# Expert gathers of a two-block transformer kernel: one token tile after the other, with blocks of 32 columns on TensorE in place of VectorE sums

## The reference, cut to what matters

```python
s1, i1 = lax.top_k(sc[:, :, 0], 16)
s2, i2 = lax.top_k(sc[:, :, 1], 16)
cand = s1[..., :, None] + s2[..., None, :]          # 16 x 16 sums a head
top_s, pos = lax.top_k(cand, 16)
idx = take_along_axis(i1 * 128 + i2, pos)           # 256 tokens x 8 heads x 16
gate = softmax(top_s)
act = gelu(einsum('chkd,cd->chk', u[idx], h))       # a dot product a row
out = einsum('chk,chkd->cd', gate * act, v[idx])    # a weighted sum of rows
x = x + out
```

## Time and profile before

| | |
|---|---|
| median of three runs | 2830.98 us |
| the profiled execution: first to last instruction | 2833.1 us |
| expert stage, first u gather to the last add into `x` | 515.6 to 1336.3 us |
| GpSimd busy over the whole span | 820.1 us |
| VectorE busy | 1396.1 us |
| TensorE busy | 2141.6 us |
| mean granted TensorE clock | 0.873 of full speed |

### The profile page before, as it was taken

How to read it: one execution, slowest core, us unless ns; L and a number is a source line. 1 busy time by engine, 2 the same in 40 slices (tenths; PEclk the granted TensorE clock), 3 DMA queues, 4 the chain that set the end, 5 groups by cost and what they waited for, 6 DMA issues and landing times. The chain is left out here.

```text
span 2833.1 us, 25536 instructions
## 1 busy us (share of the span) xinstructions
PE 2141.6 (76%) x9580; PEld 1041.9 (37%) x9580; DVE 1396.1 (49%) x2952; ACT 424.9 (15%) x914; POOL 820.1 (29%) x902
## 2 busy tenths in 40 slices
PE   7976797867836656655999799988889986655664
PEld 5544343734412222222655333322236453222222
DVE  3478434979997677776564422211146443101011
ACT  1322100112200211111222301000011131000000
POOL 3325433548777677775010000000000000000000
PEclk9986898978967777778999899999999997788778
DMA  9989999889999999998656499999995439999998
GB/s 350 405 304 364 412 413 346 309 336 390 384 372 360 341 358 365 367 357 327 232 184 228 180 410 409 409 409 409 409 390 214 178 149 345 408 409 409 409 409 320
DMA packets 297260, 975.96 MB, mean 344 GB/s; under 512 B 22833, under 2 KB 23985, under 8 KB 297009
## 3 DMA queue, kind: packets, MB, share of 16 engines
q1 hardware_dynamic: 182930, 562.20, 51.2%
q0 software_dynamic: 114208, 412.14, 38.6%
HBM read 902.97 MB, written 71.30 MB: 344 GB/s over the span
## 5 line engine op out<-in xcount | busy, mean ns | idle before, releaser
L2683 PE MATMUL ps<-big 128*32 128x256 f32 (+1 forms) x4608 | 592.3, 524 | 195.5 <-DMA big<-in_moe_w_up_dram 71.6
L498 PE MATMUL ps<-big 128*128 128x512 f32 (+3 forms) x1648 | 540.9, 492 | 31.1 <-issue 9.9
L2014 PE MATMUL ps<-big 128*128 128x512 f32 x512 | 325.5, 778 | 217.1 <-ACT big L2032 129.3
L2683 PEld LDWEIGHTS ps<-big 128*32 128x32 f32 (+1 forms) x4608 | 222.3, 135 | 548.0 <-issue 275.4
L498 PEld LDWEIGHTS ps<-big 128*128 128x128 f32 (+1 forms) x1648 | 304.6, 192 | 252.9 <-issue 223.0
L2066 DVE SCALAR_TENSOR_TENSOR big<-big 128x1024 f32<-128x1024 f32 x256 | 313.7, 1227 | 100.4 <-DMA big<-peer_rows,big 86.1
L1965 POOL DMA_INDIRECT big<-in_peer_v_dram,big x256 | 312.6, 1221 | 131.7 <-issue 75.5
L1958 POOL DMA_INDIRECT big<-peer_rows,big x256 | 278.3, 1087 | 98.9 <-issue 75.0
L2014 PEld LDWEIGHTS ps<-big 128*128 128x128 f32 x512 | 114.8, 242 | 392.6 <-issue 241.7
L2799 DVE TENSOR_TENSOR big<-big,ps 128x512 f32<-128x512 f32 (+1 forms) x32 | 17.8, 555 | 458.8 <-issue 439.9
L727 POOL DMA_DIRECT2D peer_rows<-big x256 | 149.6, 592 | 284.8 <-DVE big L739 284.3
(11 more groups left out here) (383 smaller groups left out, 2027.6 us busy)
## 6 DMA issues: line engine op xcount, KB each, us to landing
big<-in_moe_w_gate_dram SPq DMA_DIRECT2D x61, 2048.0 KB, 23.8
big<-in_moe_w_up_dram SPq DMA_DIRECT2D x61, 2048.0 KB, 23.9
big<-in_moe_w_down_dram SPq DMA_DIRECT2D x60, 2048.0 KB, 23.8
big<-in_peer_u_t_dram POOLq DMA_DIRECT2D x64, 1024.0 KB, 12.9
peer_rows<-big POOLq DMA_DIRECT2D x256, 256.0 KB, 8.3
big<-in_ada_w_dram SPq DMA_DIRECT2D x24, 2048.0 KB, 11.1
big<-in_mlstm_w_in_dram SPq DMA_DIRECT2D x12, 2048.0 KB, 15.1
big<-in_w_in_dram SPq DMA_DIRECT2D x8, 2048.0 KB, 19.5
```

The costliest lines, as they stand in the source:

```text
L498: last = pe.matmul(bank(i) if t.groups == 1 else k.ps[row:row + t.m, i % banks, 0:t.n], lhsT, rhs, start=(j < t.groups), stop=(j >= len(t. ...
L2014: last = pe.matmul(k.ps[:, 4 + 2 * t + half, :], diag[n // 2 % 4], v_buf[n % NV][:, 512 * half:512 * half + 512], start=(n < PER and n % G ...
L2683: last = pe.matmul(k.ps[q * M:q * M + M, bank, 0:W], lhsT(kc), weights_at(i, c, q * W), start=(kc == 0), stop=(kc == C - 1), skip_group_ch ...
```

## The change

- The tiles are done one after the other: groups 0 to 7 are the heads of tile 0, 8 to 15 those of tile 1. `group` selects for one head of one tile, in eleven steps; the steps are spread over all dots up to some 239 (one after each of the first 16 dots, then after two dots of three).
- `h2` of the current tile stands in the PSUM banks 6 and 7, where `turn_rows_of` puts it, and the dots read it there. For tile 1 it is put there when dot 127 is done.
- A `v` gather no longer takes one slot of 128 tokens but 8 tokens x 16 slots. The indices and weights are brought into this order by a product on VectorE, a 16-column matmul and a copy by ScalarE (`tensor_index`, `scalar_index`, `w_wide`, `w_back`). TensorE then sums all 256 `v` gathers: ScalarE builds for each a block of 128 x 32, and four blocks go to four groups of 32 output columns, so that four gathers fill the 128 partitions of the output (banks 4 and 5).
- `accumulate` is gone; the sum of a tile is added to `x` once (`add`, for tile 0 after dot 149, for tile 1 at the end). `v` buffers come free by fours.
- The context moves to three banks; `LAG` is 18, its convolution is spread over twice as many slots, the scan keeps its slots but has one output bank.

```diff
+    def group(self, dve, j, scored, spread):
...
+        t, head = divmod(j, PEER_HEADS)
+        mine = slice(K * j, K * j + K)
+        for s in range(2):
+            scored(dve, 2 * head + s, t)
+            yield from self.best(dve, self.vals[:, s], self.inds[:, s], self.sc[:, t, 2 * head + s, :], self.rest)
...
+        st(dve, dve.scalar_tensor_tensor(out=self.wide, in0=i1, scalar=float(PEER_KEYS), in1=i2, op0=ALU.mult, op1=ALU.add))
+        spread(dve, j, self.wide).then_inc(self.placed, 1)
+        dve.wait_ge(self.placed, j + 1)
...
-    NU, NV, G = 8, 8, PEER_TOPK
+    NU, NV, G, Q = 8, 8, PEER_TOPK, 4
...
+    h2 = k.ps[:, 6:8, :].rearrange("p b n -> p (b n)")
...
-    mods, LAG = ctx.mods, 20
+    mods, LAG = ctx.mods, 18
...
     def fetch_v(pool, n):
-        if n >= NV:
-            pool.wait_ge((out_done, summed)[n % 2], (n - NV) // 2 + 1)
+        if n >= NV and n % Q == 0:
+            pool.wait_ge(out_done, (n - NV) // Q + 1)
...
             if n >= G:
+                if n % G == 0:
+                    pool.wait_ge(index_kept, n // G)
                 fetch_v(pool, n - G)
...
+    def tensor_index(pe, j):
+        pe.wait_ge(sel.placed, j + 1)
+        if j == 1:
+            pe.wait_ge(index_kept, 1)
+        if j >= 2:
+            pe.wait_ge(w_kept, j - 1)
+        at = 256 + G * (j % 2)
+        pe.matmul(k.ps[:, 0, at:at + G], index_wide[j % 2], sixteenth, start=True, stop=True).then_inc(index_full, 1)
+    def scalar_index(act, j):
+        act.wait_ge(index_full, j + 1)
+        at = 256 + G * (j % 2)
+        act.activation(v_index[j % 4], k.ps[:, 0, at:at + G], ACT.Copy).then_inc(index_kept, 1)
...
+    def turn_rows_of(pe, src):
+        for half in range(2):
+            out = k.ps[:, 6 + half, :].rearrange("p (q c w) -> p c q w", q=2, c=C)
+            for c in range(C):
+                last = pe.matmul(out[:, c], src[:, c, :], k.ident[:, 64 * half:64 * half + 64], start=True, stop=True,
+                                 skip_group_check=True)
+        last.then_inc(h_full, 1)
...
     def tensor_part(pe):
         pe.wait_ge(*k.shared["tile_free"].at(len(tiles)))
+        tensor_index(pe, 0)
+        for j in range(GROUPS):
+            t = j // PEER_HEADS
+            if j == PEER_HEADS - 1:
+                pe.wait_ge(dotted, P)
+                pe.wait_ge(h_saved, 1)
+                turn_rows_of(pe, h2b)
+            if j + 1 < GROUPS:
+                tensor_index(pe, j + 1)
+                pe.wait_ge(index_kept, j + 2)
+            pe.wait_ge(w_ready, j + 1)
+            at = 288 + G * (j % 2)
+            pe.matmul(k.ps[:, 0, at:at + G], w_wide, sixteenth, start=True, stop=True).then_inc(w_full, 1)
+            if j == PEER_HEADS:
+                pe.wait_ge(added, 1)
+            for r in range(G // Q):
+                n0 = G * j + Q * r
+                pe.wait_ge(block_made, n0 + Q)
+                for n in range(n0, n0 + Q):
+                    pe.wait_ge(v_loaded[n % NV], 16 * (n // NV + 1))
+                for half in range(2):
+                    for q in range(Q):
+                        last = pe.matmul(k.ps[32 * q:32 * q + 32, 4 + half, :], blocks[j % 2][:, Q * r + q, :],
+                                         v_buf[(n0 + q) % NV][:, 512 * half:512 * half + 512],
+                                         start=(j % PEER_HEADS == 0 and r == 0),
+                                         stop=(j % PEER_HEADS == PEER_HEADS - 1 and r == G // Q - 1), skip_group_check=True)
+                last.then_inc(out_done, 1)
+                for n in range(n0, n0 + Q):
+                    ctx.tensor(pe, n + LAG)
...
     def scalar_part(act):
+        scalar_index(act, 0)
+        sel.scalar_exp(act, 0)
+        for j in range(GROUPS):
+            act.wait_ge(dotted, G * (j + 1))
+            act.activation(gelus[:, G * j:G * j + G], dots[:, G * j:G * j + G], ACT.Gelu).then_inc(gelu_done, 1)
+            if j + 1 < GROUPS:
+                scalar_index(act, j + 1)
+                sel.scalar_exp(act, j + 1)
+            at = 288 + G * (j % 2)
+            act.wait_ge(w_full, j + 1)
+            act.activation(w_back[j % 2], k.ps[:, 0, at:at + G], ACT.Copy).then_inc(w_kept, 1)
+            act.wait_ge(w_kept, j + 1)
+            if j >= 2:
+                act.wait_ge(out_done, G // Q * (j - 1))
+            for c in range(G):
+                act.activation(blocks[j % 2][:, c, :], placer[:, c // Q, :], ACT.Copy, scale=w_back[j % 2][:, c:c + 1])\
+                   .then_inc(block_made, 1)
+                if c % Q == Q - 1:
+                    for n in range(G * j + c - Q + 1, G * j + c + 1):
+                        ctx.scalar(act, n + LAG)
...
-        def accumulate(n):
...
+        def weigh(j):
+            dve.wait_ge(sel.exped, j + 1)
+            st(dve, dve.reciprocal(sel.inv, sel.sums))
+            dve.wait_ge(gelu_done, j + 1)
+            mine = slice(G * j, G * j + G)
+            st(dve, dve.scalar_tensor_tensor(out=w, in0=gelus[:, mine], scalar=sel.inv, in1=sel.gate[:, mine],
+                                             op0=ALU.mult, op1=ALU.mult))
+            if j:
+                dve.wait_ge(w_full, j)
+            wide_of(dve, w_wide, w).then_inc(w_ready, 1)
+        def add(t):
+            dve.wait_ge(out_done, (t + 1) * P // Q)
+            x = k.x[:, t, :].rearrange("p (b n) -> p b n", b=2)
+            dve.tensor_tensor(x, x, k.ps[:, 4:6, :], ALU.add).then_inc(added, 1)
...
+        places(dve)
+        for _ in sel.group(dve, 0, scored, spread_index):
+            pass
+        ahead = (step for j in range(1, GROUPS) for step in sel.group(dve, j, scored, spread_index))
         for n in range(N):
+            if n % P == 0:
+                dve.wait_ge(h_full, n // P + 1)
             dve.wait_ge(u_loaded[n % NU], 16 * (n // NU + 1))
             u = u_buf[n % NU]
+            dve.scalar_tensor_tensor(out=u, in0=u, scalar=1.0, in1=h2, op0=ALU.mult, op1=ALU.mult,
+                                     accum_out=dots[:, n:n + 1]).then_inc(dotted, 1)
             if n >= G and n % G == 1:
                 weigh(n // G - 1)
+            ctx.vector(dve, n)
+            if n < G or n % 3 < 2:
                 next(ahead, None)
+            if n == P + G + 5:
+                add(0)
+        weigh(GROUPS - 1)
+        add(1)
```

More of the change, by code:

```diff
@@ L1304, in __init__ @@
[L1304 to L1310 removed]
+        self.one_hot = work(k, 2048, 512).rearrange("p (s n m) -> p s n m", s=2, n=K)
```

308 lines of the change are left out of this document (101 added, 207 removed).

## The result

The changed kernel took 2857.74 us (median of six, 2853.28 to 2864.43) beside 2830.82 for the kernel before: 1.0088 times, interval 1.0065 to 1.0111. That is slower by 27 us, where 17 less were forecast. Later comparisons qualify it. A second one gave 1.0067 (1.0046 to 1.0088). A third gave **0.9953** (0.9938 to 0.9968), and there the kernel before took 2805.95 us itself. The sign goes with how fast gathers run on the chip at the time.

What follows compares the result with a forecast made beforehand. GpSimd, its gathers held off by VectorE instructions, was taken as the bound of the expert stage. Terms -10 - 25 + 2 + 6 + 9 + 1 = -17 us gave 2814 us, range 2786 to 2856 us.

Steps and rivals of the forecast that it cites:

- Term 1: Gathers at 800 to 930 and 963 to 1310 us: GpSimd's holds end, DMA engines become the bound; -10 and -25 us.
- the rival in which they do not end: GpSimd's gathers: long ones have another cause, rate stays at 361 GB/s, only costs remain, +18, 2849 us; chance 0.11.
- Terms 4, 5 and 6: Expert stage: start, later first v gathers, +2 us; change of tiles, dot 128 waiting, +6; new waits behind it, +9.
- Term 4: Start of the expert stage: v(0) waits for indices from TensorE behind the last score tile; +2 us, bounds -5 and +13.
- Term 7: End of the expert stage: four gathers' matmuls and one add stand after the last landing; +1 us.
- Terms 2 and 3: Expert stage: VectorE's work, 86% busy, stays hidden; TensorE's sums fit, barely at the lower clock; no term for either.
- The late chain: VectorE's scan waits for maxima from TensorE, which runs later; +20 on the sum, 2834 us, no change; chance 0.17.
- The rival that I named in half a sentence: Objection to the rival of an always-full gather queue (2792 us, chance 0.20): v buffers freed by fours; no own chance.

Runs made afterwards that it cites:

- e4: Changed kernel with ScalarE copying h2 of each tile to SBUF, where the dots read it; 2850.59 us, 1.0072 times the kernel before.
- e6: Changed kernel with dots over 128 of the 1024 columns, gathers whole; 2853.33 us, one run.
- e5: Changed kernel with tile 0's sums added behind dot 143 instead of 149; 2854.53 us, 1.0082 times the kernel before.
- e7: Changed kernel with tile 1's h2 rows turned at the start and read in SBUF; 2858.41 us, 1.0094 times the kernel before.
- e10: Changed kernel with the first 16 slots' v indices turned behind the 25th score tile instead of the last; 2848.60 us, 1.0070 times the kernel before.

## Why the prediction was wrong, step by step

**Term 1, -35 us, failed.** The step was "less than the 2.70 of the DMA engines, which become the bound", at 389 GB/s. Its first half was right: the long gathers were holds, they went with the `ps` operand, and the rival in which they do not end is refuted by the means. The rule of the Trainium skill ("SBUF — State Buffer", "Who interferes with whom") on two SBUF inputs agrees with that. Its inference that descriptor generation goes untouched is not settled: gathers of 0.94 us lasted up to 2.00 beside such instructions, but the hold may lie in the read of the indices alone.

The second half failed. With GpSimd free, gathers alone did not go at 389 GB/s but at 359 (1045 to 1300 us, 2.92 us a pair for 2.70), and the 35 us came out as 2.9 (-3.0 and +0.1 in the table). They went at 352 with the holds (e4) and at 362 with VectorE nearly free (e6). GpSimd had read as full (348 of 347 us) beside a DMA share of 0.96, and I took the first for the bound. The share was the sign: the same packets at a full share give an estimated 376 GB/s (361 / 0.96), 14 us where I wrote 25. The 389 of 640 to 800 us was with weights among the gathers and was no promise for gathers alone in these conditions. What stood in the place of the holds were waits for `v` buffers, most of them for late signals, a term that my sum did not have. How much of the pace is the DMA engines' own and how much the signals' stays open.

**With fast gathers the sign is that of the forecast.** The changed kernel then has 404 and 378 GB/s in the stretches of term 1 and is 12.9 us faster than the kernel before; the sum said 17. That is no confirmation: the sum was made from a profile in usual conditions, and no term of it can be measured against the kernel before there. That GpSimd's holds bound that kernel with fast gathers is argued, not shown. The kernel before moved by only 23 us between the conditions (2828.76 to 2805.95), the changed one by 55 (2847.74 to 2793.10).

**Terms 4, 5 and 6** have their size in the table above: +2 was -1.6, +6 was +5.1, +9 was +6.6. The wait before dot 128 was said to be 21 us and is 20.42; v(0) at 578.91 is before the 580 named. Term 4 misread one thing in the kernel before: TensorE's 7.46 us were not shown to be a wait for query weights. ScalarE stood for a signal of matmuls that were over at 562.53, and TensorE went on behind its copy:

```profile
569.46 0.38 ACT L2088 ACTIVATE big<-ps 128x256 f32<-128x256 f32 x1 [10.29 <-remote]
```

As separate prices the terms mean less than they seem: e5, e7 and e10 took single stops away and gained nothing that shows, and only several together did.

**Term 7, +1, was +6.5.** I counted the last sums and the add, and not that only `v` gathers are left, at most eight, freed by fours; that this is the cause is argued. The 8 us between dots 24 and 40 were in no term: GpSimd stood 9.00 us for the third four sums there and 8.38 for the fourth.

**Terms 2 and 3** held in that neither engine became the bound. Four gathers take 1.92 us at the full clock and 3.64 at the lower, where 3.5 and 7 were feared, and the dot with a `ps` operand 1219 ns for 1229. VectorE is busy 248 of 347 us, 72% for the 86% feared. The late chain came with another cause: VectorE's scan line L1569 waited 23.3 us in 963 to 1310 us, up to 6.7 in one piece, but 20.2 of them for late signals. With fast gathers the line waits 6.2 us.

**The rival that I named in half a sentence** ("v buffers come free by fours, which leaves two or three pairs under way") describes the waits in the profile, but freeing them finer did not pay. Whether a finer release that keeps the four groups side by side would pay stays open.

## What to carry to other kernels

An engine that reads 100% busy beside DMA engines at 0.96 is not thereby the bound: shorten its work in an experiment (short operands, whole transfers) and see whether the rate moves. Take the rate that DMA engines can reach from a stretch with the same kind of transfer. Where an engine waits, look whether the work that it waits for had long ended. And time the kernel before in every comparison: here its own 1% between comparisons was the sign of conditions under which the change turns from 0.7% slower to 0.5% faster.

## What the runs showed of the hardware

- One program gathered at 362 GB/s with dips every 23 us in one profile and at 406 nearly without them in another (1100 to 1200 us). The cause is open.
- In the profiles with dips, signals between engines came late: v(184) started 5.2 us after the end of the sums that it needed, VectorE waited 2.29 us for its own instruction before, and in e10 ScalarE started 12.6 us after the end of the matmuls. Such waits stand in all sixteen profiles with slower gathers and in none of the four with fast ones.
- A gather that is issued beside VectorE instructions with two SBUF operands took 1043 and 1188 ns in the mean, and 954 and 948 once the dots read one operand in PSUM.
- Sixteen records of 128x512 on four column groups took 1.92 or 3.64 us, by the level of the clock. The same work a gather at a time cost 0.30 us a record instead of 0.22, from 1045 to 1300 us.
- A version with five edits (early index and first group, add at dot 143, tile 1's rows copied into PSUM by ScalarE, sixteen v gathers at the end, context norm four slots later) is 1.3% faster than the kernel before where gathers are fast. Without the last of these edits it is 0.2% slower where they are not; the whole was not timed there.
